# Feed-forward gate and up products with the weights stationary and 256 tokens moving

## What is computed

```python
def rmsnorm(x, g):
    xf = x.astype(jnp.float32)
    y = xf * lax.rsqrt(jnp.mean(xf * xf, axis=-1, keepdims=True) + EPS)
    return (y * g.astype(jnp.float32)).astype(x.dtype)
...
        hn = rmsnorm(h, g_ffn[l])
        gu = jnp.einsum('bsd,df->bsf', hn, w_gate_up[l])
        act = jax.nn.silu(gu[..., :D_FF]) * gu[..., D_FF:]
        h = h + jnp.einsum('bsf,fd->bsd', act, w_down[l])
...
        h = h + 0.5 * rmsnorm_2(swiglu(rmsnorm_2(h, g[0]), ffn_w_gu[l, 0], ffn_w_down[l, 0]), g[1])
```

## Time and profile before

| what | value |
| --- | --- |
| median of 3 runs | 1395.73 us (1394.19 to 1405.68) |
| the profiled execution, first to last instruction | 1394.8 us |
| TensorE busy | 1350.5 us, 97% of the span |
| VectorE busy | 767.0 us, 55% |
| ScalarE busy | 656.1 us, 47% |
| GpSimd busy | 92.3 us, 7% |
| share of TensorE in the chain that ended last | 92% |
| DMA, mean over the span | 169 GB/s |

### The profile page before, as it was taken

The page is one execution under the profiler, slowest core; times in us unless marked ns, Lnnn a source line. Parts: engine busy times, 40 slices in busy tenths (PEclk is TensorE's granted clock), DMA queues, the critical chain, the costliest instruction groups (busy, mean ns, idle before and its releaser), DMA issues.

```text
span 1394.8 us, 17017 instructions
## 1 busy us (share of the span) xinstructions
PE 1350.5 (97%) x6155; PEld 1101.7 (79%) x6155; DVE 767.0 (55%) x863; ACT 656.1 (47%) x924; POOL 92.3 (7%) x154
## 2 busy tenths in 40 slices
PE   6999989999999999999999999999999998999998
PEld 5777768888888888788788887888888766788886
DVE  5662556545464554667655456555445645754554
ACT  5553545344454344545633444553443644644333
POOL 4231100000000000010100001000000201100000
PEclk9995999999999999999999999999999989999999
DMA  9440336555656555464665555555555430565551
GB/s 322 158 169 0 122 91 211 180 181 190 193 167 191 193 181 183 149 216 148 205 201 180 181 196 180 181 180 182 181 189 195 143 121 1 180 215 192 180 180 61
DMA packets 163469, 236.03 MB, mean 169 GB/s; under 512 B 7728, under 2 KB 120552, under 8 KB 163424
## 3 DMA queue, kind: packets, MB, share of 16 engines
q1 hardware_dynamic: 160864, 228.62, 50.2%
q0 software_dynamic: 1840, 4.64, 1.0%
q10 hardware_dynamic: 720, 2.17, 0.4%
HBM read 234.35 MB, written 1.05 MB: 169 GB/s over the span
## 4 chain that ended last, share of the span: by engine, by line
PE 92%; ACT 3%; DVE 3%; DMA 2%; issue 1%; POOL 0%; SPq 0%; DVEq 0%; POOLq 0%; ACTq 0%
PE B L1246 20%; PE B L1248 20%; PE B L1247 20%; PE B L1526 7%; PE B L1528 7%; PE B L1527 7%; PE T L1539 2%; PE B L1669 1%; DMA w_raw<-in_w_in 1%; PE B L1409 1%; DVE w_lo L821 1%; ACT w_hi L486 1%; DMA w_raw<-in_w_mem_kv 1%; ACT xt_hi L499 1%; ACT junk L508 1%
## 5 line engine op out<-in xcount | busy, mean ns | idle before, releaser
L821 DVE TENSOR_TENSOR w_lo<-w_raw,w_hi 128x2048 fp32r<-128x2048 f32 x217 | 498.1, 2297 | 310.3 <-ACT w_hi L486 310.3
L1246 PE MATMUL B<-w_hi,xt_lo 128*128 128x512 f32 x1296 | 518.0, 400 | 14.4 <-DVE xt_lo L836 13.9
L1248 PE MATMUL B<-w_hi,xt_hi 128*128 128x512 f32 x1296 | 508.0, 392 | 0.0
L1247 PE MATMUL B<-w_lo,xt_hi 128*128 128x512 f32 x1296 | 506.7, 391 | 0.0
L486 ACT ACTIVATE w_hi<-w_raw 128x2048 fp32r<-128x2048 f32 x217 | 415.2, 1914 | 180.2 <-PE B L1528 131.1
L1246 PEld LDWEIGHTS B<-w_hi,xt_lo 128*128 128x128 f32 x1296 | 245.0, 189 | 68.5 <-issue 10.5
L1248 PEld LDWEIGHTS B<-w_hi,xt_hi 128*128 128x128 f32 x1296 | 244.4, 189 | 52.8
L1247 PEld LDWEIGHTS B<-w_lo,xt_hi 128*128 128x128 f32 x1296 | 245.2, 189 | 47.4
L1526 PE MATMUL B<-w_hi,act_lo 128*128 128x512 f32 x400 | 156.1, 390 | 0.0
L1528 PE MATMUL B<-w_hi,act_hi 128*128 128x512 f32 x400 | 155.6, 389 | 0.0
L1527 PE MATMUL B<-w_lo,act_hi 128*128 128x512 f32 x400 | 155.6, 389 | 0.0
(11 more groups left out here) (230 smaller groups left out, 789.2 us busy)
## 6 DMA issues: line engine op xcount, KB each, us to landing
w_raw<-in_ffn_w_gu SPq DMA_DIRECT2D x176, 512.0 KB, 4.7
w_raw<-in_ffn_w_down SPq DMA_DIRECT2D x88, 512.0 KB, 3.9
w_raw<-in_w_gate_up SPq DMA_DIRECT2D x44, 512.0 KB, 4.7
w_raw<-in_conv_w_in SPq DMA_DIRECT2D x24, 512.0 KB, 4.5
w_raw<-in_w_down SPq DMA_DIRECT2D x22, 512.0 KB, 3.7
w_raw<-in_w_in SPq DMA_DIRECT2D x16, 512.0 KB, 4.8
w_raw<-in_w_kv SPq DMA_DIRECT2D x16, 512.0 KB, 4.8
w_raw<-in_w_mem_kv SPq DMA_DIRECT2D x8, 512.0 KB, 12.8
```

The costliest lines, as they stand in the source:

```text
L821: dve.tensor_tensor(wlo[slot][:, :], raw[slot][:, :], whi[slot][:, :].bitcast(F32), ALU.subtract)\
L1246: pe.matmul(bank[:, :], xlo[:, k, x], whi[s][:, c], start=first, stop=False)
L1247: pe.matmul(bank[:, :], xhi[:, k, x], wlo[s][:, c], start=False, stop=False)
L1248: return pe.matmul(bank[:, :], xhi[:, k, x], whi[s][:, c], start=False, stop=last)
```

## The change

For blocks 1 to 10 of each feed-forward the operands change places: 128 weight columns are stationary and the 256 tokens of xT move. `GU[0]` then holds the gate, `GU[1]` the up sums of the block, feature-major, as two chunks of 256 tokens. Block 0 stays as it was, and is turned.

The norm's rstd now belongs to columns instead of partitions. Once per feed-forward ScalarE writes two diagonal matrices of rstd, TensorE multiplies them by ones, which gives a row of rstd on all partitions in `T[1]`, and ScalarE copies it out (`rb`). VectorE multiplies the gate sums by it (`gate_T`), ScalarE takes silu (`silu_T`), VectorE multiplies by the up sums (`act_T`), ScalarE and VectorE write hi and lo (`act_T_hi`, `act_T_lo`). The up sums are not scaled: the down sums are, later, in `h_update` and `post_update`, and through the scale of the squares. The order of splits and activations on both queues is new.

```diff
@@ ScalarE @@
+                def silu_T(n):
+                    act.wait_ge(gs_ok, n + 1)
+                    act.activation(gate_f, gate_s, ACT.Silu).then_inc(si_ok, 1)
+                def act_T_hi(n, hi=ahi[:, :]):
+                    act.wait_ge(fa_ok, n + 1)
+                    act.activation(hi, act_f, ACT.Copy).then_inc(act_hi, 1)
...
                 split_at(u0 + 3)
                 act.wait_ge(rstd, 2 * ST[stat] + 2)
-                gate_of(0, u0 + 1, PAIR[0])
-
-                def step(i, last):
-                    split(v + 3 * i + 2, (v + 2) % RING, i + (v + 2) // RING)
-                    act_out(i)
+                rstd_diag()
+                gate_tok()
+                split_at(v + 2)
+                rstd_row_out()
+                act_tok_hi()
+                def step(i):
                     split(v + 3 * i + 3, (v + 3) % RING, i + (v + 3) // RING)
-                    gate_of(i + 1, v + 3 * i + 1, GU)
-                    if not (last and v + 3 * i + 4 >= UNITS):
-                        split(v + 3 * i + 4, (v + 4) % RING, i + (v + 4) // RING)
+                    silu_T(n0 + i)
+                    split(v + 3 * i + 4, (v + 4) % RING, i + (v + 4) // RING)
+                    act.wait_ge(w_used, v + 3 * i + 3)
+                    act_T_hi(n0 + i)
+                    split(v + 3 * i + 5, (v + 5) % RING, i + (v + 5) // RING)
...
-                step(FJ - 2, True)
-                act_out(FJ - 1, last_hi)
-                split_at(u0 + 34)
+                split_at(u0 + 32)
+                silu_T(n0 + FJ - 2)
+                act_T_hi(n0 + FJ - 2, last_hi)
+                split_at(u0 + 33, u0 + 34)
@@ VectorE @@
+                def gate_T(n, u):
+                    dve.wait_ge(w_used, u + 1)
+                    dve.tensor_tensor(gate_s.rearrange("p (k t) -> p k t", k=2),
+                                      GU[0][:, :].rearrange("p (k t) -> p k t", k=2),
+                                      rb.unsqueeze(1).to_broadcast([P, 2, S]), ALU.mult).then_inc(gs_ok, 1)
+                def act_T(n):
+                    dve.wait_ge(si_ok, n + 1)
+                    dve.tensor_tensor(act_f, GU[1][:, :], gate_f, ALU.mult).then_inc(fa_ok, 1)
...
+                def step(i):
+                    gate_T(n0 + i, v + 3 * i + 1)
                     split(v + 3 * i + 3, (v + 3) % RING)
-                    act_of(i + 1, GU)
+                    act_T(n0 + i)
+                    split(v + 3 * i + 4, (v + 4) % RING)
+                    act_T_lo(i + 1)
+                    split(v + 3 * i + 5, (v + 5) % RING)
...
+                gate_T(n0 + FJ - 2, u0 + 30)
+                split_at(u0 + 32)
+                act_T(n0 + FJ - 2)
+                act_T_lo(FJ - 1, last_hi, last_lo)
+                split_at(u0 + 33, u0 + 34)
@@ TensorE @@
                 def up_unit(u, slot, k0):
                     pe.wait_ge(w_lo, u + 1)
                     for k in range(k0, k0 + 4):
-                        for t in range(TOKS):
-                            ins = product(GU[t], slot, columns(k), k, t, k == 0, k == KD - 1)
+                        for c in range(4):
+                            w = slice(k % 4 * HALF + c * P, k % 4 * HALF + c * P + P)
+                            o = GU[c // 2][:, c % 2 * S:c % 2 * S + S]
+                            pe.matmul(o, whi[slot][:, w], xlo[:, k, :], start=k == 0 and c % 2 == 0, stop=False)
+                            pe.matmul(o, wlo[slot][:, w], xhi[:, k, :], start=False, stop=False)
+                            ins = pe.matmul(o, whi[slot][:, w], xhi[:, k, :], start=False,
+                                            stop=k == KD - 1 and c % 2 == 1)
                     ins.then_inc(w_used, 1)
...
+                up_unit(v, v % RING, 0)
+                rstd_row()
+                turn_act()
+                up_unit(v + 1, (v + 1) % RING, 4)
...
-                def step(i, first):
-                    up(i, first)
+                def step(i):
+                    pe.wait_ge(fa_ok, n0 + i)
+                    up_unit(v + 3 * i, v % RING, 0)
+                    up_unit(v + 3 * i + 1, (v + 1) % RING, 4)
                     down_ready(v + 3 * i + 2, i)
...
-                turn_act(FJ - 1)
```

More of the change, by code:

```diff
@@ L674, in ffn, with rstd_diag @@
                        (lambda t: h_squares(stat, reader, t)) if squares else lambda t: None, k0)
[L676 to L679, removed]
+                def rstd_diag():
                     for t in range(TOKS):
-                        act.activation(gate[:, t, :], pair[t][:, 0:256], ACT.Silu,
-                                       scale=RS[:, ST[stat], t:t + 1]).then_inc(gate_ok, 1)
@@ L684, in act_out, with gate_tok @@
-                def act_out(j, hi=ahi[:, :]):
-                    act.wait_ge(act_t, FJ * f + j + 1)
-                    act.activation(hi, T[0][:, :], ACT.Copy).then_inc(act_hi, 1)
+                        act.activation(rdiag[:, t * P:t * P + P], ident[:, :], ACT.Copy,
+                                       scale=RS[:, ST[stat], t:t + 1]).then_inc(rd_ok, 1)
+                def gate_tok():
+                    act.wait_ge(w_used, u0 + 2)
+                    if f:
+                        act.wait_ge(act_t, f)
+                    for t in range(TOKS):
+                        act.activation(gate[:, t, :], PAIR[0][t][:, 0:256], ACT.Silu,
+                                       scale=RS[:, ST[stat], t:t + 1]).then_inc(gate_ok, 1)
@@ L1065, in ffn @@
+                n0 = (FJ - 1) * f
                 split_at(u0 + 3)
-                dve.wait_ge(rstd, 2 * ST[stat] + 2)
-                act_of(0, PAIR[0])
-                def step(i, last):
-                    split(v + 3 * i + 2, (v + 2) % RING)
-                    act_out(i)
+                act_tok()
+                split_at(v + 2)
+                act_tok_lo()
+                dve.wait_ge(rb_ok, f + 1)
+                def step(i):
+                    gate_T(n0 + i, v + 3 * i + 1)
                     split(v + 3 * i + 3, (v + 3) % RING)
-                    act_of(i + 1, GU)
-                    if not (last and v + 3 * i + 4 >= UNITS):
-                        split(v + 3 * i + 4, (v + 4) % RING)
+                    act_T(n0 + i)
+                    split(v + 3 * i + 4, (v + 4) % RING)
+                    act_T_lo(i + 1)
+                    split(v + 3 * i + 5, (v + 5) % RING)
@@ L1533, in down_ready, with rstd_row, turn_act @@
                     pe.wait_ge(act_lo, FJ * f + j + 1)
-                def turn_act(j):
-                    pe.wait_ge(act_ok, 2 * (FJ * f + j) + 2)
+                def rstd_row():
+                    pe.wait_ge(rd_ok, 2 * f + 2)
+                    pe.wait_ge(ones_ok, 1)
+                    for t in range(TOKS):
+                        ins = pe.matmul(T[1][:, t * P:t * P + P], ones[:, :], rdiag[:, t * P:t * P + P], start=True,
+                                        stop=True)
+                    ins.then_inc(rb_done, 1)
+                def turn_act():
+                    pe.wait_ge(act_ok, 2 * f + 2)
                     for k in range(2):
@@ L1543, in ffn @@
                 v = u0 + 2
-                def up(i, first):
-                    if not first:
-                        pe.wait_ge(act_ok, 2 * (FJ * f + i) + 2)
+                n0 = (FJ - 1) * f
+                up_unit(v, v % RING, 0)
+                rstd_row()
+                turn_act()
+                up_unit(v + 1, (v + 1) % RING, 4)
+                down_ready(v + 2, 0)
+                for t in range(TOKS):
+                    for half in range(2):
+                        ins = down((v + 2) % RING, t, half, True)
+                ins.then_inc(w_used, 1)
+                def step(i):
+                    pe.wait_ge(fa_ok, n0 + i)
                     up_unit(v + 3 * i, v % RING, 0)
-                    turn_act(i)
                     up_unit(v + 3 * i + 1, (v + 1) % RING, 4)
-                def step(i, first):
-                    up(i, first)
                     down_ready(v + 3 * i + 2, i)
```

87 lines of the change are left out of this document (62 added, 25 removed).

## The result

| | before | changed |
| --- | --- | --- |
| median of 15 runs each, on the same chip | 1397.91 us | 1409.49 us |
| ratio to before, 95% interval | | 1.0064 (1.0043 to 1.0085) |
| the profiled execution | 1394.8 us | 1408.2 us |

The change makes the kernel slower, by 0.64%. That is inside 1%, but its interval is clear of one, the direction is the other one than forecast, and the time lies above the forecast range (1373 to 1403 us). The 15 runs of the changed kernel lie between 1407.5 and 1411.3 us, those of the kernel before between 1393.6 and 1406.4.

What follows compares the result with a forecast made beforehand. TensorE was taken to bound the kernel. From 1394.8 us, 17.3 saved, 2.2 added for the rstd row, 1.9 given back at ends and 0.7 for multiplications gave 1382.3, as a median 1383 us; range 1373 to 1403 us.

Steps and rivals of the forecast that it cites:

- Reading the bound: Whole kernel: TensorE, busy 97% of the span, sets the time; other engines' work counts only where TensorE waits.
- What goes: Blocks 1 to 10, five feed-forwards: fifty turnings of 0.45 us leave TensorE's path, 22.5 us.
- The exchange of operands: Gate/up products: 4800 matmuls of 256 columns at 0.1146 us replace 2400 of 512; with turnings gone, 17.3 us saved.
- the rival that the loads show: Gate/up matmuls of 256 columns stand 0.116 to 0.121 us apart, giving 1390 to 1414 us; chance 0.18.
- The point of decision: Gate/up products: at a 256-column distance of 0.1172 us the gain is gone; each nanosecond is 4.8 us.
- Half of m: m is the 0.227 us between 512-column matmuls; half, 0.1135, was the better rival's pace, 1378 us; chance 0.12.
- No overlap: Rival in the gate/up products: load and matmul do not overlap, 0.227 us, about 1920 us; chance 0.02.
- The handover: Between gate/up products: VectorE and ScalarE finish in 3.9 us beside a 5.45 us down product, so no stall.
- The branches: Rival: the longer TensorE loop body causes instruction fetches at 35 taken branches, 1383 to 1547 us, put at 1418; chance 0.04.
- What is added: The row of rstd on TensorE, once per feed-forward: 0.44 us, five times, 2.2 us.
- The ends: Feed-forward ends: later splits delay the update of h; 1.9 us given back plus 0.7 us for longer multiplications.
- What would show it: Profile signs: 256-column matmuls 0.114 to 0.115 us apart, steps of 16.45 us, idle time at four ends grown 0.2 to 0.5.

Runs made afterwards that it cites:

- e1_wide: The changed kernel with gate/up products of blocks 1 to 10 put back to 2400 matmuls of 512 columns, output wrong: ratio to before 0.9863, span 1377.5 us.
- e3_load64: The changed kernel loading only 64 of each 128 weight columns in gate/up products of blocks 1 to 10, output wrong: span 1374.4 us, distance 113 ns.
- e4_move192: The changed kernel moving only 192 of 256 tokens in gate/up products of blocks 1 to 10, full loads, output wrong: span 1381.8 us, distance 111 ns.
- e7_early_split: The changed kernel with ScalarE's split of unit u0 + 33 moved ahead of the last block's hi part, output unchanged: ratio to before 1.0067.
- e10_slopes_later: The changed kernel with the early split of u0 + 33 and GpSimd's eight slope writes moved behind the fourth feed-forward's row statistic: ratio to before 1.0026.

## Why the prediction was wrong, point by point

- **Reading the bound.** Right. TensorE set the end before and after, without a pause in the steps, and the loss is found in its distances and at four ends, less what the attention stretch gave back.
- **What goes, 22.5 us.** Right: a step of `e1_wide` is 0.465 us shorter than one before the change, fifty are 23 us.
- **The exchange of operands.** This is the step that failed: "I take 0.1146, as the forget-gate row is the nearest in type, width and operand". The row was near in all but the weight load, 8 columns instead of 128. The term was mis-sized by 4800 x 5.4 ns = 26 us: the distance is 0.120. That this is the forecast's whole error (1382.3 against 1408.2) is chance, since the ends cost 4.0 us more than forecast and the attention stretch 4.6 less. The bounds had the truth in them: 0.112 to 0.121, and the rival that the loads show gave 1403 to 1413 us at 0.119 to 0.121. I gave it 0.18. It is what came, as `e3_load64` shows: with half the load 6.5 ns of the distance go. The point of decision, 0.1172, follows from the sum, but with ends of 6.6 us it would lie at 0.1164. (The times for 0.1135 and 0.112, 1378 and 1371 us, are medians, 1377 and 1370 as spans; those for 0.119 and 0.121 are spans.)
- **A sign that I passed over.** "Half of m would be 0.1135" takes the 227 ns as proportional to the columns. It holds a fixed 13.7 ns (227 - 512 / 2.4), which doubling the count doubles. The 0.11 us at the end of rows 4 was one load behind one matmul. In `e4_move192` the first distance behind the 512-column matmuls is 0.08 or 0.09 us at the start of every product, where the steady distance is 0.111. One pair does not show a steady pace.
- **No overlap.** Rightly held very unlikely: a full load and a 256-column matmul together take 0.120 us, not 0.227. The rule under "The mechanism" in Part 3 of "TensorE: Matmul & The Clock Gate" (the Trainium skill) does not describe these loads.
- **The handover.** Right: 3.5 us measured, 3.9 forecast, 5.45 at hand.
- **The branches.** Right: 33 instruction packets instead of 28, and no gap in the windows.
- **What is added.** The row of rstd costs 223.80 to 224.24 in the timeline, 0.44 us, as forecast.
- **The ends.** Right in kind, too small in size: 6.6 us where I had 2.6. The idle time before the turning of h grew by 0.34, 0.96, 0.97 and 2.05 us, where the sign named was 0.2 to 0.5. Summed over the four ends, TensorE's idle time around the turning grew from 4.4 to 7.6 us. Most of the other 3.3 us are matmuls at half the clock at the second and fourth end, which the forecast did not consider. The fourth end's own cause was missed: GpSimd's slope writes stand in the queue ahead of the statistic there.
- **What would show it.** The sign named for this case, "steps of 16.8 us or more with TensorE busy mean that the loads show", is what the profile has.

## What to carry to other kernels

Where TensorE is the bound, count matmuls as well as columns: here each one with a full load cost 13 ns over its columns, so an exchange of operands that halves the moving side has to pay 13 ns for each matmul that it adds, and one that drops 50 turnings did not. Take the price of a matmul from a row with the same load and the same moving size in a long row of its kind, not from a sum of single hidden loads. And when a step gets shorter on TensorE, look at what stands in the queues at the ends of the stage: here the place of one split and of eight small writes decided some 3 us of idle time at four ends, and in the profiles compared 6 us with the slow clock behind it. And take such a sum apart stage by stage before a total that agrees is believed: here two differences of 4 us and more cancelled.

## What the runs showed of the hardware

- From 256 to 512 columns moved, matmuls in the rounded type with 128 columns loaded stand 13.3 to 13.7 ns (11.7 at 288) plus 0.417 ns a column apart; at 192 to 240 a full load holds the distance at 111 to 112 ns. The Trainium skill, "TensorE: Matmul & The Clock Gate", "Back-to-back issue gap", gives the columns at 2.4 GHz plus 2.5 ns for a matmul by itself; no row here comes down to that in this type, and an estimate by it (109 ns for 256 columns) is 11 ns short.
- A narrow load is no help at 384 and 512 columns. At 512 it was even 4 ns slower (231 against 227).
- The granted clock fell to its 1.2 GHz level behind the second and the fourth end of the changed kernel, with 1.78 and 3.10 us of idle time before the turning. The windows (clock in the last column but two):

```profile
584.00:587.50 3.50, 1.71 (x10) 1.05 (x9) 2.94 (x6) 2.33 (x8) 1.93 (x4) 0.93 1.02 389
587.50:591.00 3.50, 3.50 (x12) 2.63 (x11) 3.46 (x11) 2.73 (x10) 0.67 (x3) 0.58 0.52 183
1112.00:1116.00 4.00, 0.90 (x6) 0.42 (x4) 2.74 (x5) 1.67 (x5) 3.59 (x10) 1.00 1.04 360
1116.00:1119.40 3.40, 3.39 (x11) 2.62 (x11) 2.87 (x11) 3.31 (x12) 0.37 (x1) 0.51 0.71 246
```

  The length of that idle time does not decide it. The third end has 1.78 us as well and keeps the full clock. In `e7_early_split` the clock fell at the second end, with 1.06 us, and not at the fourth, with 2.43:

```profile
583.35:592.32 8.97, 7.50 (x29) 5.42 (x27) 6.91 (x15) 4.95 (x16) 1.82 (x5) 0.81 0.45 168
1110.38:1119.04 8.66, 5.91 (x29) 4.28 (x27) 6.85 (x16) 5.06 (x16) 4.69 (x10) 1.00 0.63 224
```

  Where it fell in the changed kernel, the slow matmuls cost some 1.5 us on top of the idle time. `e10_slopes_later` keeps the full clock at all four ends; what decides it is not shown here, so its 28.1 us at the ends may be luck in part.
- GpSimd's 128 x 128 writes took 1.3 us each beside VectorE's splits and 0.3 us each behind them (5.23 and 1.31 us for four).
